# Feed-forward output of a two-layer trunk: column blocks 0 and 1 by seven block products for two chunks, blocks 2 and 3 summed over two chunks in PSUM

## What is computed

```python
def conv_glu_ffn(x, w_in, conv_w, conv_b, w_out):
    S = x.shape[1]
    h = x @ w_in                                  # 2048 -> 2 * 5632: gate and value
    hp = jnp.pad(h, ((0, 0), (CONV_WIDTH - 1, 0), (0, 0)))
    hc = conv_b + hp[:, 0:S] * conv_w[0]
    for kk in range(1, CONV_WIDTH):
        hc = hc + hp[:, kk:kk + S] * conv_w[kk]
    gate, val = jnp.split(hc, 2, axis=-1)
    return (jax.nn.gelu(gate, approximate=False) * val) @ w_out
...
        x = layer_norm(DEEPNORM_ALPHA * x + mix, ...)
        x = layer_norm(DEEPNORM_ALPHA * x + conv_glu_ffn(x, ...), ...)
```

## Time and profile before

| | |
|---|---|
| median of three runs | 2062.64 us |
| profiled execution, span from the first to the last instruction | 2061.1 us |
| outside the span (median less span) | 1.5 us |
| TensorE matmul busy | 2052.3 us |
| TensorE weight load busy | 1756.3 us |
| VectorE busy | 1444.6 us |
| ScalarE busy | 887.1 us |
| bytes moved | 389.57 MB |

### The profile page before, as it was taken

How to read it: one execution, slowest core, us unless ns; L and a number is a source line. 1 busy time by engine, 2 the same in 40 slices (tenths; PEclk the granted TensorE clock), 3 DMA queues, 4 the chain that set the end, 5 groups by cost and what they waited for, 6 DMA issues and landing times.

```text
span 2061.1 us, 27212 instructions
## 1 busy us (share of the span) xinstructions
PE 2052.3 (100%) x10924; PEld 1756.3 (85%) x10924; DVE 1444.6 (70%) x1641; ACT 887.1 (43%) x825; POOL 5.8 (0%) x10
## 2 busy tenths in 40 slices
PE   9999999999999999999999999999999999999998
PEld 8888888888888888888888877888888888888887
DVE  5446566767767687677697886786776768766768
ACT  5433443543443434434434555354344344444342
POOL 0000000000000000000000000000000000000000
PEclk9999999999999999999999999999999999999999
DMA  9654474655555565555555435465555555555552
GB/s 331 196 191 145 142 258 163 235 197 187 188 196 186 187 198 184 186 199 184 188 186 190 144 123 190 162 241 194 194 184 193 193 184 195 191 184 195 191 184 102
DMA packets 194766, 389.57 MB, mean 189 GB/s; under 512 B 6970, under 2 KB 9748, under 8 KB 193684
## 3 DMA queue, kind: packets, MB, share of 16 engines
q1 hardware_dynamic: 194419, 388.49, 56.6%
q10 hardware_dynamic: 288, 0.26, 0.1%
HBM read 386.36 MB, written 2.10 MB: 188 GB/s over the span
## 4 chain that ended last, share of the span: by engine, by line
PE 98%; DVE 1%; DMA 0%; SPq 0%; issue 0%; ACT 0%; DVEq 0%
PE ps L1270 36%; PE ps L1280 19%; PE ps L1297 13%; PE ps L1299 12%; PE ps L1298 12%; PE ps L1420 1%; PE ps L1711 1%; PE ps L1686 1%; PE ps L1694 1%; PE ps L1387 0%; PE ps L1425 0%; PE ps L1258 0%; PE ps L1537 0%; DMA xres<-x 0%; DVE xres L810 0%; PE ps L1338 0%
## 5 line engine op out<-in xcount | busy, mean ns | idle before, releaser
L475 ACT ACTIVATE w_hi<-raw 128x2048 fp32r<-128x2048 f32 x352 | 673.9, 1916 | 951.1 <-DMA raw<-ffn_w_in 523.7
L752 DVE TENSOR_TENSOR w_lo<-raw,w_hi 128x2048 fp32r<-128x2048 f32 x352 | 800.9, 2287 | 220.0 <-ACT w_hi L475 219.2
L1270 PE MATMUL ps<-T,w_hi 128*128 128x512 f32 x3264 | 765.0, 390 | 0.0
L1270 PEld LDWEIGHTS ps<-T,w_hi 128*128 128x128 f32 x3264 | 605.7, 188 | 122.9 <-issue 1.7
L1280 PEld LDWEIGHTS ps<-T,w_lo 128*128 128x128 f32 x3264 | 405.8, 192 | 10.0 <-issue 2.0
L1280 PE MATMUL ps<-T,w_lo 128*128 128x256 f32 x3264 | 410.6, 283 | 0.0
L1297 PE MATMUL ps<-w_hi,gT 128*128 128x512 f32 x704 | 274.2, 389 | 0.0
L1299 PE MATMUL ps<-w_hi,gT 128*128 128x512 f32 x704 | 273.9, 389 | 0.0
L1298 PE MATMUL ps<-w_lo,gT 128*128 128x512 f32 x704 | 273.9, 389 | 0.0
L782 DVE TENSOR_TENSOR arena<-ps,half 128x512 f32<-128x512 f32 x96 | 65.5, 688 | 183.6 <-ACT half L539 183.6
L786 DVE SCALAR_TENSOR_TENSOR xres<-ps,xres 128x1024 f32<-128x1024 f32 (+1 forms) x103 | 117.9, 1144 | 89.1 <-PE ps L1299 87.9
(11 more groups left out here) (159 smaller groups left out, 802.9 us busy)
## 6 DMA issues: line engine op xcount, KB each, us to landing
raw<-ffn_w_in SPq DMA_DIRECT2D x176, 1024.0 KB, 5.0
raw<-ffn_w_out SPq DMA_DIRECT2D x88, 1024.0 KB, 5.0
raw<-even_w_in SPq DMA_DIRECT2D x38, 1024.0 KB, 5.1
raw<-attn_w_qkv SPq DMA_DIRECT2D x20, 1024.0 KB, 5.2
raw<-even_w_out SPq DMA_DIRECT2D x16, 1024.0 KB, 5.0
raw<-attn_w_out SPq DMA_DIRECT2D x16, 1024.0 KB, 5.1
arena<-ln_gain SPq DMA_DIRECT2D x4, 1024.0 KB, 6.3
arena<-ln_bias SPq DMA_DIRECT2D x4, 1024.0 KB, 8.3
```

Source lines behind the costliest of these rows:

```text
L475: nc.scalar.activation(w_hi[:, s % RING], raw[:, s % RING], ACT.Copy).then_inc(hi_ready, 1)
L752: vec.tensor_tensor(w_lo[:, s % RING], raw[:, s % RING], w_hi[:, s % RING].bitcast(F32), ALU.subtract).then_inc(lo_ready, 1)
L1270: ins = mm(ps[:, banks[j]], w_hi[:, s % RING, k, P * j:P * j + P], T[:, GK * kg + k], start=kg == 0 and k == 0, stop=kg == KG - 1 and k == ...
```

## The change

Chunks 2p and 2p+1 make a duo (p = 0 to 4); chunk 10 stays alone. For output blocks 0 and 1 the duo's product is a 2 by 2 block product (token halves by chunks, times chunks by column blocks). It is now made of seven products of 12 matmuls where eight were. TensorE needs 8 forms of the gated chunks (4 plain, 4 sums) with high and low parts, and 7 weight groups: 3 loaded as they are, 4 sums made on VectorE, one of them (`SUM_24`) in place of a loaded group. All 7 get a high and a low part. Blocks 2 and 3 are summed over the duo's two chunks in PSUM and added to `xres` once. The hardware loop is gone. The order is now G0 V0 G1 V1 and, for each duo, G(2p+2) V(2p+2), the quad (7 products), G(2p+3) V(2p+3), C(p) (4 groups, blocks 2 and 3); in the last duo C4 follows the quad, and then chunk 10's 4 output groups (tail). The load of the norm's gain and bias now waits for the last quad, since `lnp` holds three of the weight sums. The copies of the convolution's taps to `cur` (L1022) are gone.

```diff
+SUM_12, W_11, W_22, SUM_24, SUM_124, W_21, SUM_ALL = range(PRODUCTS)
...
-            def load(s, source, turn=0):
-                if not isinstance(turn, int) or s >= RING:
-                    sp.wait_ge(used, s - RING + 1 + turn * 12)
-                sp.dma_start(raw[:, s % RING], source).then_inc(raw_landed[s % RING], 16)
+            def load(s, source):
+                i = LOAD_OF[s]
+                if i >= RING:
+                    sp.wait_ge(used, SLOT_OF[i - RING] + 1)
+                sp.dma_start(raw[:, i % RING], source).then_inc(raw_landed[i % RING], 16)
...
+                for p in range(DUOS):
+                    a, b = 2 * p, 2 * p + 1
+                    chunk(a + 2)
+                    q, s = base + Q_AT[p], base + C_AT[p]
+                    out_block(l, q + W_11, a, 0)
+                    out_block(l, q + W_22, b, 1)
+                    out_block(l, q + SUM_24, a, 1)
+                    out_block(l, q + W_21, b, 0)
+                    if b + 2 < FC:
+                        chunk(b + 2)
+                    for i in range(KG):
+                        out_block(l, s + i, (a, b)[i % 2], 2 + i // 2)
+                for n in range(NCH):
+                    if n == 2:
+                        sp.wait_ge(used, base + Q_AT[DUOS - 1] + PRODUCTS)
+                        load_params(2 * l + 1)
+                    out_block(l, base + TAIL_AT + n, FC - 1, n)
...
+                def weight_sums(p):                       # VectorE
+                    dve.wait_ge(*landed(q + W_11))
+                    dve.wait_ge(*landed(q + SUM_24))
+                    (SUM_12 = W_11 + raw of SUM_24)
+                    dve.wait_ge(*landed(q + W_22))
+                    (SUM_24 = its raw + W_22;  SUM_124 = SUM_12 + W_22)
+                def last_weight_sum(p):
+                    (SUM_ALL = SUM_124 + W_21)
+                def take_product(p, i, bank, a, n, sign, before=0):
+                    if before:
+                        dve.wait_ge(quad_read, r + before)
+                    vec.scalar_tensor_tensor(xres[:, a, c], ps[:, bank], sign / ALPHA, xres[:, a, c],
+                                             ALU.mult, ALU.add).then_inc(quad_read, 1)
...
+                    s = base + V_AT[a]                    # VectorE, V(2p+2)
+                    for j in range(KG):
+                        if j < 2:
+                            gate_pair(a, j, x)
+                        if j == 1:
+                            weight_sums(p)
+                        low(s + j + LO_LEAD)
+                    s = base + Q_AT[p]                    # the quad
+                    low(s + LO_LEAD)
+                    dve.wait_ge(used, s + 1)
+                    last_weight_sum(p)
+                    take_product(p, 0, x, 1, 1, -1.0)
+                    low(s + 1 + LO_LEAD)
+                    dve.wait_ge(used, s + 2)
+                    take_product(p, 1, x + 1, 0, 0, 1.0)
+                    low(s + 2 + LO_LEAD)
+                    dve.wait_ge(used, s + 3)
+                    take_product(p, 2, x, 0, 1, -1.0)
+                    low(s + 3 + LO_LEAD)
...
+                    (takes 3 to 8, each after its product; then low(s + 5 + LO_LEAD), low(s + 6 + LO_LEAD))
...
+                s = base + C_AT[DUOS - 1]                 # VectorE, C4
+                for j in range(KG):
+                    if j == 2:
+                        dve.wait_ge(used, s + 2)
+                        add_chunk(2, 0, ffn_added)
+                    low(s + j + LO_LEAD)
+                    if j < 2:
+                        value_pair(c, j, 4)
+                    else:
+                        gated_low(j - 2)
...
+                def quad(p, x):                           # TensorE
+                    pe.wait_ge(form_ready, FORMS * (DUOS * l + p + 1))
+                    ready(s)
+                    form_product(s + SUM_12, D_1, x, True).then_inc(used, 1)
+                    ready(s + W_11)
+                    form_product(s + W_11, X_11, x + 1, True).then_inc(used, 1)
+                    ready(s + W_22)
+                    pe.wait_ge(quad_read, r + 1)
+                    form_product(s + W_22, D_4, x, False, more=True).then_inc(used, 1)
+                    ready(s + SUM_24)
+                    form_product(s + SUM_24, D_3, x + 3, True).then_inc(used, 1)
+                    ready(s + SUM_124)
+                    pe.wait_ge(quad_read, r + 2)
+                    form_product(s + SUM_124, D_2, x + 1, False, more=True).then_inc(used, 1)
+                    (then W_21 with X_12 in bank x + 2, and SUM_ALL with X_22 added in bank x + 3 after quad_read r + 4)
```

More of the change, by code:

```diff
@@ L52 @@
 U_HALVES = {6: (1, 0), 7: (0, 1)}
-ARENA = 14080
+ARENA = 14864
+FRONT = 8720
 RING = 6
@@ L113 @@
 BURSTS = PAIRS + 3
-TURNS = FC - 2
-LOOP_OWN = 12
 class Count:
     def __init__(self):
[L122 to L132, removed]
+        self.n = 0
 def build_trunk(nc, x, ln_gain, ln_bias, even_w_in, pool_w, pool_scale, even_w_out, attn_w_qkv, attn_b_qkv,
@@ L342, in even_in, with hidden @@
                 load(s, w_even_in[:, GK * kg:GK * kg + GK, cols(EVEN_COLS[c])])
-            def hidden(l, s, c, value, turn=0):
+            def hidden(l, s, c, value):
                 for kg in range(KG):
[L346 to L351, removed]
+                    load(s + kg, w_ffn_in[l][:, GK * kg:GK * kg + GK, cols(c * COLS + value * D_FF)])
@@ L353, in ffn, with out_block @@
+            def out_block(l, s, c, n):
+                load(s, w_ffn_out[l][:, GK * c:GK * c + GK, cols(n * COLS)])
             def ffn(l):
                 base = S_FFN[l]
[L355 to L373, removed]
+                def chunk(c):
+                    hidden(l, base + G_AT[c], c, 0)
+                    hidden(l, base + V_AT[c], c, 1)
@@ L528, in norm_fill, with halves @@
                     norm_high(m, u)
-            def halves(n, bank, ended, turn=0):
+            def halves(n, bank, ended):
                 if n == TP_ODD + 7:
@@ L659, in feed_forward @@
[L659 to L666, removed]
-                    if j in (1, 2):
[L668 to L672, removed]
+                        chunk_gelu(0, j - 6)
@@ new lines, in feed_forward @@
+                tail, c = base + TAIL_AT, FC - 1
+                s = base + C_AT[DUOS - 1]
+                for j in range(KG):
+                    if j == 2:
+                        dve.wait_ge(used, s + 2)
+                        add_chunk(2, 0, ffn_added)
+                    low(s + j + LO_LEAD)
+                    if j < 2:
+                        value_pair(c, j, 4)
+                    else:
+                        gated_low(j - 2)
+                dve.wait_ge(used, tail)
+                add_chunk(3, 2, ffn_added)
@@ L1605, in turn_gate, with hidden @@
                     ins.then_inc(gate_turned, 1)
-                def hidden(s, bank, turn=0, waits=(), gate=False):
+                def hidden(at, bank, waits=(), gate=False):
+                    s = base + at
                     for kg in range(KG):
```

519 lines of the change are left out of this document (359 added, 160 removed).

## The result

The changed kernel takes **2068.95 us** (median of six runs, 2067.41 to 2071.07) against 2062.63 us for the kernel before on the same chip (2062.47 to 2062.76): ratio 1.0032, 95% interval 1.0020 to 1.0043. It is slower. The forecast was 2057.6, the range 2048 to 2066, and "slower" had been given one chance in ten. The profiled execution took 2067.41 us with a span of 2065.6, so 1.8 us lie outside the span.

A forecast was written before the change was run, and what follows sets the result against it. TensorE, busy in all of the span, was taken as the bound. Its terms: 2061.1 - 27.2 (matmuls) + 16.4 (quads) + 5.8 (tail) = 2056.1, with 1.5 outside the span 2057.6 us; range 2048 to 2066.

The forecast's parts named there:

- What is removed from TensorE: In five duos and two layers, eight products of 12 matmuls become seven: 120 matmuls fewer, 27.2 us off the path.
- The quad's queue: In each quad, eight VectorE instructions after `SUM_24` lands delay take 0, so product 2 waits: 1.64 us, 16.4 for ten.
- the restart: In each quad, TensorE starts product 2 0.05 us after take 0 ends; a further 0.11 goes to its first matmuls.
- The margins behind it: VectorE's lows and takes queued behind take 0 are not late: low of `SUM_124` done at 31.3, product due at 34.7.
- The tail: After C4 in the last duo, TensorE waits 2.9 us for the gated low, twice in the kernel: 5.8 us.
- Unit prices: Costs read from the earlier trace: output matmuls 0.2267 us each, a product of 12 matmuls 2.72 us.
- two bounds for the price of a sum: On VectorE, a weight sum costs 2.20 us, as in a run of lows, or 2.287, a lone low; 2.20 taken.
- rival C: Granted clock falls to 1.2 GHz at TensorE's quad and tail waits; one product of 12 slowed each gives 2090; chance 0.07.
- Rival A: The quads do not wait, as take 0 comes 1.5 us earlier: 2041 us; with times up to the forecast, chance 0.12.
- rival B: VectorE's sums and lows do not overlap and cost 2.287 us each: 2065.5 us, no measurable change; chance 0.12.
- Rival D: TensorE also waits elsewhere, where margins are smallest, up to 0.5 us a quad: 2063 us; chance 0.09.

## Why the prediction was wrong, point by point

- **What is removed from TensorE** (-27.2): right. 10804 matmuls, and an eighth product costs 27.0 to 27.8.
- **The quad's queue** (+16.4): right in mechanism and in size (16.5 by the run with take 0 first). VectorE idle until the landing, a pitch of 2.20, take 0 behind the last sum, and TensorE behind take 0 are all in the trace; the restart of 0.15 was written down as 0.05. The margins behind it held.
- **The tail** (+5.8): right mechanism, 5.1 measured.
- **Unit prices: the step that failed.** "Output matmuls: 81 of them lie between 608.64 and 627.00, 0.2267 each" was read from matmuls with `gT` as the stationary operand and then used for matmuls from `forms`, a tile that the kernel before does not have. They take 0.234, and slow the ones behind them. The missing term is 8.5 us net (10.3 of pace, less 1.8 that would otherwise be waited). It alone takes the forecast from 2057.6 to 2066.1, past the 2062 that the forecast allowed for itself and to the end of the whole range. No row of before could have given it: there `T` and `gT` both lie right from `w_hi` and `w_lo`, by luck, and the earlier trace rows is the price of a lucky place. The prediction took two bounds for the price of a sum; for the matmuls from `forms` it took one figure and named no rival with another.
- **The clock** (rival C, chance 0.07): it happened, in the small and not in every execution. I worked it out for a whole product in each of the twelve waits; in the traces it was eight matmuls, 0.20 more each (0.227 was written down), behind none, one or both of the tail's waits and behind none of the quads': 0 to 3.4 us, about 1.5 in the median.
- **Rival A** fell with the waits, **rival B** with the pitch of 2.20 in the quad. The sentence that the prediction quotes from the Trainium skill (VectorE: DVE Perf Modes, The DRAIN you can't avoid) would have had at least 2.29 there; the row disagrees, for sums as for lows. **Rival D** did not show: the list has no third wait of size.

The account, on profiled executions: 2062.6 - 27.2 + 16.5 + 5.1 + 8.5 = 2065.5, against 2067.4. The 1.9 us left over have the size of what the terms hide from each other: each was measured by taking it out alone, and taking out the slow pace lengthened the waits by 1.8. With the pace at its full 10.3 the sum is 2067.3.

## What to carry to other kernels

A unit price belongs to its tiles as well as to its shape: if a change brings a new stationary or moving tile, look up where it will lie, and put it a multiple of 256 bytes from the tiles that it is multiplied with; here that is worth 8.5 us of 2067 in the changed kernel, and a wrong place would cost 14.7 of 2063 in the one before. What a faster pace gives back is capped by the other engine's queue: 3.4 us where VectorE's last take was next. When an engine that is full gets a shorter program, follow the other engine's queue in front of each bank it must free: a take of 0.6 us behind a sum of 2.2 us gave back 60% of seven-for-eight, and swapping the two lines got it back. A wait of TensorE of 2 us can cost more than itself, since the clock may fall behind it.

## What the runs showed of the hardware

- A matmul of 512 columns (fp32r, weights moving) follows the one before after 0.2267 us when its stationary and its moving tile lie a multiple of 256 bytes apart in a partition, and after about 0.234 when they lie 32, 64, 96 or 128 bytes beyond one (128 a little cheaper: 2075.8 against 2077.0 to 2077.6). `gT` and `forms` were tried at bytes from 132224 to 214144; only the distance told. Distances that are no multiple of 32 were not tried. The cause inside the chip is open: the runs show the rule, not the mechanism. In the traces the weight loads (188 ns) overlap the matmuls, so that a clash of two reads would fit, but nothing here shows it.
- The slower pace outlasts the slow tile by about six matmuls (`gT` behind `forms`, 0.232 and then 0.227).
- The granted clock fell to 1.2 GHz within 2 us of the end of waits of TensorE of 2.0 to 2.4 us, at 8 of the 16 such waits in the traces (at one tail and not at the other of the same execution in six of them), and was back after eight matmuls. In the traces of the three kernels without these waits it did not.
